# A sixth of a conditioning product moved from the first stage to the routing stage, in plain f32, and a first norm scaled in four chunks

## What is computed

```python
mod = jax.nn.silu(c) @ w_ada + b_ada            # c: 9 vectors of 2048; w_ada: 2048 x 12288
sh1, sc1, gt1, sh2, sc2, gt2 = split(mod, 6)
h  = rms_norm(x, g_pre_mix) * (1 + sc1) + sh1   # the first norm
z  = h @ w_in                                   # then gated linear attention, a conv branch, and a merge: mix
x  = x + gt1 * rms_norm(mix, g_post_mix)
h2 = rms_norm(x, g_pre_ffn) * (1 + sc2) + sh2
f  = peer(h2, ...)                              # product keys: top 16 of 128 twice, top 16 of their sums, experts
x  = x + gt2 * rms_norm(f, g_post_ffn)
```

## Time and profile before

| what | value |
|---|---|
| median of 3 runs | 5565.51 us (5557.96, 5565.51, 5580.36) |
| profiled execution, span from first to last instruction | 5572.9 us |
| profiled execution's own time | not listed apart; of the three runs only 5580.36 us is as long as that span, 7.5 us above it |
| PE, DVE, ACT, POOL busy | 90%, 61%, 31%, 25% of the span |
| bytes moved by DMA | 1334.66 MB, 239 GB/s on average |
| first stage | 0 to about 342 us |
| routing stage | about 2970 to 3209 us |

### The profile page before, as it was taken

The page is one execution under the profiler, slowest core; times in us unless marked ns, Lnnn a source line. Parts: engine busy times, 40 slices in busy tenths (PEclk is TensorE's granted clock), DMA queues, the critical chain, the costliest instruction groups (busy, mean ns, idle before and its releaser), DMA issues. The chain is left out here.

```text
span 5572.9 us, 61778 instructions
## 1 busy us (share of the span) xinstructions
PE 5025.0 (90%) x23369; PEld 4105.5 (74%) x23369; DVE 3416.3 (61%) x4470; ACT 1727.9 (31%) x2279; POOL 1402.2 (25%) x1059
## 2 busy tenths in 40 slices
PE   8989999999998888989793589999999999978885
PEld 3347888888886545868683589999999889866774
DVE  7842211115675243222558968888888778878898
ACT  6843112122223111122424623333333233323332
POOL 0500000000100131000004723333434333444453
PEclk9989999999999899989897899999999999999998
DMA  9842322233333355432511699999999999999998
GB/s 362 321 155 89 104 96 99 88 104 101 114 101 119 133 205 192 154 109 90 168 38 35 147 350 382 394 376 379 374 373 380 370 377 372 388 381 406 407 400 347
DMA packets 460055, 1334.66 MB, mean 239 GB/s; under 512 B 135868, under 2 KB 193084, under 8 KB 377198
## 3 DMA queue, kind: packets, MB, share of 16 engines
q1 hardware_dynamic: 336180, 667.06, 33.9%
q0 software_dynamic: 96576, 623.69, 28.5%
q10 hardware_dynamic: 27072, 40.91, 2.1%
HBM read 1206.06 MB, written 126.56 MB: 239 GB/s over the span
## 5 line engine op out<-in xcount | busy, mean ns | idle before, releaser
L229 PE MATMUL ps<-w_hi,act_hi 128*128 128x512 f32 x3040 | 1202.0, 395 | 36.6 <-DVE w_lo L224 16.3
L230 PE MATMUL ps<-w_lo,act_hi 128*128 128x512 f32 x3040 | 1191.9, 392 | 0.0
L231 PE MATMUL ps<-w_hi,act_lo 128*128 128x512 f32 x3040 | 1191.7, 392 | 0.0
L224 DVE TENSOR_TENSOR w_lo<-w_stage,w_hi 128x2048 fp32r<-128x2048 f32 x152 | 348.2, 2291 | 1134.6 <-ACT w_hi L220 1133.8
L2436 ACT ACTIVATE x_hi<-x_stage 128x1024 fp32r<-128x1024 f32 x512 | 543.4, 1061 | 1504.8 <-DMA x_stage<-u_turned 707.5
L2526 DVE TENSOR_TENSOR x_lo<-x_stage,x_hi 128x1024 fp32r<-128x1024 f32 x512 | 626.2, 1223 | 368.7 <-ACT x_hi L2436 368.1
L2363 POOL DMA_INDIRECT u_ring<-u_exp,idx_all x256 | 597.1, 2332 | 844.4 <-DVE u_ring L2544 801.5
L2390 PE MATMUL ps<-act_hi,x_hi 128*128 128x384 f32 x2048 | 697.3, 340 | 60.2 <-DVE x_lo L2526 57.4
L2390 PE MATMUL ps<-x_hi,cx_hi 128*128 128x512 f32 x1536 | 611.8, 398 | 99.7 <-DVE cx_lo L2537 82.8
L229 PEld LDWEIGHTS ps<-w_hi,act_hi 128*128 128x128 f32 x3040 | 576.2, 190 | 162.0 <-issue 32.1
L2391 PE MATMUL ps<-act_lo,x_hi 128*128 128x384 f32 x2048 | 694.4, 339 | 0.0
(11 more groups left out here) (315 smaller groups left out, 5637.3 us busy)
## 6 DMA issues: line engine op xcount, KB each, us to landing
x_stage<-u_turned SPq DMA_DIRECT2D x256, 512.0 KB, 8.6
x_stage<-v_exp SPq DMA_DIRECT2D x256, 512.0 KB, 9.3
w_stage<-w_ada SPq DMA_DIRECT2D x96, 1024.0 KB, 6.1
w_stage<-w_in SPq DMA_DIRECT2D x96, 1024.0 KB, 5.2
d_w<-w_buf SPq DMA_DIRECT2D x6, 4096.0 KB, 20.7
gwr<-d_w SPq DMA_DIRECT2D x128, 192.0 KB, 10.6
d_gw<-gob ACTq DMA_DIRECT2D x128, 192.0 KB, 6.9
gwr<-d_gw SPq DMA_DIRECT2D x128, 192.0 KB, 10.3
```

Of the source, the lines that this page charges most:

```text
L224: dve.tensor_tensor(w_lo[:, q % 2], w_in_st[:, q], w_hi[:, q % 2].bitcast(F32), ALU.subtract).then_inc(w_split, 1)
L229: pe.matmul(out, lhs[0], rhs[0], start=first, stop=False)
L230: pe.matmul(out, lhs[0], rhs[1], start=False, stop=False)
L231: return pe.matmul(out, lhs[1], rhs[0], start=False, stop=last)
```

## The change

The first stage makes 20 chunks, not 24, in the order first shift, first scale, second shift, second scale, first gate (`PARTS`, `place`). The first norm's scaling is packed into chunks 14 to 17, four blocks in each. SCALE2 moves to chunk 16. The conditioning vectors, after silu, are stored to DRAM (`d_c`).

The routing stage makes the last sixth: four chunks of 512 columns, each in eight halves of a quarter (`HALVES` = 32; a half is 256 rows x 512 columns, 512 KB). PE multiplies the weights as they come, in plain f32, with no split by ACT or DVE: two matmuls a half, and one with a single row for the bias after each eighth half. There are two buffers, and the load of half n waits until half n - 2 was multiplied; the first load of a new chunk waits for the whole chunk before it. 24 halves stand on PE ahead of everything else of the stage, the other 8 one behind each of the first eight groups of tile 0. When all 32 are used, the gain's rows are loaded; DVE multiplies them with the sums in PSUM after its last tile, and SP writes the result to `d_post`.

```diff
-    NA = 6 * D // NCOL
+    NA = 5 * D // NCOL
+    PARTS = (0, 1, 3, 4, 2)
...
-        SCALE0, TURN0, MT, AFF0, POST1, SCALE2 = 7, 8, 10, 14, 12, 20
+        SCALE0, TURN0, MT, AFF0, SCALE2 = 7, 8, 10, 14, 16
...
-            return range(2 * (c - AFF0), 2 * (c - AFF0) + 2) if AFF0 <= c < AFF0 + KD // 2 else ()
+            return range(4 * (c - AFF0), 4 * (c - AFF0) + 4) if AFF0 <= c < AFF0 + KD // 4 else ()
+        def place(c):
+            return PARTS[c // 4] * 4 + c % 4
...
-            pool.dma_start(mod[:], a["b_ada"].broadcast_to([NSEQ, 6 * D])).then_inc(s_b, 16)
+            pool.dma_start(mod[:], a["b_ada"][:, 0:5 * D].broadcast_to([NSEQ, 5 * D])).then_inc(s_b, 16)
...
+            pool.wait_ge(s_csplit, 1)
+            pool.dma_start(d_c, c_in[:]).then_inc(s_modout, 16)
...
-            pool.dma_start(d_mod, mod[:]).then_inc(s_modout, 16)
+            pool.dma_start(d_mod[:, 0:5 * D], mod[:]).then_inc(s_modout, 16)
...
-                if not ks or j % 2 == 0:
+                if not ks:
                     return
-                k = ks[j // 2 % 2]
+                k = ks[j % QPC]
...
-                if ks and n % (2 * QPC) in (3, 6):
-                    k = ks[n % (2 * QPC) // 6]
+                at = n % (2 * QPC)
+                if ks and at in (2, 3, 5, 6):
+                    k = ks[(2, 3, 5, 6).index(at)]
...
+        G2 = 4
+        HALVES = 2 * QPC * G2
+        EARLY = 24
...
         @block.sync
         def _(sp):
+            sp.dma_start(c_all[:], d_c).then_inc(g2_c, 16)
+            for n in range(HALVES):
+                i, h = divmod(n, 2 * QPC)
+                if h == 0:
+                    if i > 0:
+                        sp.wait_ge(g2_sum, i)
+                    at = 5 * D + i * NCOL
+                    sp.dma_start(b_row[:], a["b_ada"][:, at:at + NCOL]).then_inc(g2_b, 16)
+                if n >= 2:
+                    sp.wait_ge(g2_used, n - 1)
+                src = a["w_ada"][(5 * D // NCOL + i) * QPC + h // 2]
+                sp.dma_start(wst[:, n % 2], src[:, h % 2 * (QK // 2):(h % 2 + 1) * (QK // 2), :]).then_inc(g2_in[n % 2], 16)
+            sp.wait_ge(g2_used, HALVES)
+            sp.dma_start(g_rows, a["g_post_ffn"].broadcast_to([NSEQ, D])).then_inc(g2_g, 16)
...
+            sp.wait_ge(g2_done, G2)
+            sp.dma_start(d_post, g_rows).then_inc(g2_out, 16)
...
+            sp.wait_ge(g2_out, 16)
...
+            def gate_half(n):
+                i, h = divmod(n, 2 * QPC)
+                if n == 0:
+                    pe.wait_ge(g2_c, 16)
+                pe.wait_ge(g2_in[n % 2], 16 * (n // 2 + 1))
+                for kk in range(QK // 2):
+                    k = h * (QK // 2) + kk
+                    mm = pe.matmul(ps[0:NSEQ + 1, i], c_all[:, k], wst[:, n % 2, kk], start=k == 0, stop=False)
+                mm.then_inc(g2_used, 1)
+                if h == 2 * QPC - 1:
+                    pe.wait_ge(g2_b, 16 * (i + 1))
+                    pe.wait_ge(g2_ones, 1)
+                    pe.matmul(ps[0:NSEQ + 1, i], ones[:], b_row[:],
+                              start=False, stop=True).then_inc(g2_sum, 1)
+            for n in range(EARLY):
+                gate_half(n)
             for t in range(ND):
                 turn_ids(t)
                 for q in range(NQ):
                     spread(t, q)
+                    if EARLY + t * NQ + q < HALVES:
+                        gate_half(EARLY + t * NQ + q)
...
+            dve.wait_ge(g2_sum, G2)
+            dve.wait_ge(g2_g, 16)
+            for i in range(G2):
+                g = g_rows[:, i * NCOL:(i + 1) * NCOL]
+                dve.tensor_tensor(g, ps[0:NSEQ, i], g, ALU.mult).then_inc(g2_done, 1)
```

More of the change, by code:

```diff
@@ L169, in _build @@
     d_post = d_mod[:, 5 * D:6 * D]
+    d_c = dram("d_c", (P, KD, NSEQ + 1))
     kc_at = -(-nc.sbuf_base // 32) * 32
@@ L266, in _build @@
     with stage() as (st, block):
-        c_in = sb(st, "c_in", [P, KD, NSEQ])
-        c_sig = sb(st, "c_sig", [P, KD, NSEQ])
+        c_in = sb(st, "c_in", [P, KD, NSEQ + 1])
+        c_sig = sb(st, "c_sig", [P, KD, NSEQ + 1])
         c_hi = sb(st, "c_hi", [P, KD, NSEQ + 1], F32R)
         c_lo = sb(st, "c_lo", [P, KD, NSEQ + 1], F32R)
-        mod = sb(st, "mod", [NSEQ, 6 * D])
+        mod = sb(st, "mod", [NSEQ, 5 * D])
         g9 = sb(st, "n1_g9", [NSEQ, D])
@@ L300, in _ @@
                 for q in range(QPC):
-                    load_quarter(sp, c, q, a["w_ada"][c * QPC + q])
+                    load_quarter(sp, c, q, a["w_ada"][place(c) * QPC + q])
             for q in range(QPC):
@@ L322, in _ @@
                 pool.tensor_tensor(rows_k, rows_k, by_stream[0], ALU.add).then_inc(h_sample, 1)
-            for n, name in ((1, "g_pre_ffn"), (2, "g_post_ffn")):
-                pool.wait_ge(gain_done, n + 1)
-                pool.dma_start(g9[:], a[name].broadcast_to([NSEQ, D])).then_inc(s_g9, 16)
+            pool.wait_ge(gain_done, 2)
+            pool.dma_start(g9[:], a["g_post_mix"].broadcast_to([NSEQ, D])).then_inc(s_g9, 16)
             pool.wait_ge(m2_taken, 1)
             pool.dma_start(d_mod2t, mod_t[:].rearrange("p m k s -> p (m k s)")).then_inc(s_modout, 16)
-            pool.wait_ge(gain_done, 4)
-            pool.dma_start(d_mod, mod[:]).then_inc(s_modout, 16)
-            pool.wait_ge(s_modout, 32)
+            pool.wait_ge(gain_done, 3)
+            pool.dma_start(d_mod[:, 0:5 * D], mod[:]).then_inc(s_modout, 16)
+            pool.wait_ge(s_modout, 48)
         @block.scalar
@@ L425, in extras @@
                                     ).then_inc(mt_taken, 1)
-                if c == POST1 or c == NA - 1:
-                    n, at = (1, 2 * D) if c == POST1 else (3, 5 * D)
-                    dve.wait_ge(s_g9, 16 * (n + 1))
+                if c == NA - 1:
+                    dve.wait_ge(s_g9, 48)
                     dve.wait_ge(mod_read, c + 1)
-                    dve.tensor_tensor(mod[:, at:at + D], mod[:, at:at + D], g9[:], ALU.mult).then_inc(gain_done, 1)
+                    dve.tensor_tensor(mod[:, 2 * D:3 * D], mod[:, 2 * D:3 * D], g9[:], ALU.mult).then_inc(gain_done, 1)
                 if c == SCALE2:
-                    dve.wait_ge(s_g9, 48)
+                    dve.wait_ge(s_g9, 32)
                     dve.wait_ge(mod_read, c + 1)
@@ L511, in _ @@
                 if c == SCALE2 + 1:
-                    pe.wait_ge(gain_done, 3)
+                    pe.wait_ge(gain_done, 2)
                     pe.wait_ge(m2_clear, 1)
@@ L1948, in _build, with route @@
     lk = link(None, "dve")
-    route(nc, a, stage, sem, sb, kc, ps, (idx_all, wt_all, top_all, topi_all), area, d_w, lk)
+    route(nc, a, stage, sem, sb, kc, ps, (idx_all, wt_all, top_all, topi_all), area, d_w, lk, d_c, d_post)
     experts(nc, a, stage, sem, sb, ps, (idx_all, wt_all), act_hi, act_lo, area, d_post, d_w, d_gw, d_f3, d_x2, d_h2)
-def route(nc, a, stage, sem, sb, kc, ps, route_sb, area, d_w, lk):
+def route(nc, a, stage, sem, sb, kc, ps, route_sb, area, d_w, lk, d_c, d_post):
     idx_all, wt_all, top_all, topi_all = route_sb
@@ L1992, in route @@
         w_buf = sb(st, "w_buf", [P, 2, NKEY, P // 2])
+        c_all = sb(st, "g2_c", [P, KD, NSEQ + 1])
+        wst = sb(st, "g2_w", [P, 2, QK // 2, NCOL])
+        b_row = sb(st, "g2_b", [1, NCOL])
+        ones = sb(st, "g2_ones", [1, NSEQ + 1])
+        g_rows = wst[0:NSEQ].rearrange("p a k n -> p (a k n)")
+        G2 = 4
+        HALVES = 2 * QPC * G2
+        EARLY = 24
+        g2_ones = sem("g2_onesdone")
+        g2_c, g2_b, g2_in = sem("g2_cin"), sem("g2_bin"), [sem(f"g2_in{n}") for n in range(2)]
+        g2_used, g2_sum, g2_g, g2_done, g2_out = (sem("g2_" + n) for n in ("used", "sum", "gin", "done", "out"))
+        assert nc.sbuf_base <= 229344 - 4 * (2 * TT - 3) * NH * TOPK
         s_ex, s_exd, gate, route_done = sem("r_ex"), sem("r_exd"), sem("r_gate"), sem("r_done")
@@ L2031, in _ @@
                                  w_buf[:, h]).then_inc(w_out[h], 16)
+            sp.wait_ge(g2_done, G2)
+            sp.dma_start(d_post, g_rows).then_inc(g2_out, 16)
             for h in range(2):
                 sp.wait_ge(w_out[h], 16 * ND)
+            sp.wait_ge(g2_out, 16)
         @block.gpsimd
         def _(pool):
+            pool.memset(ones[:], 1.0).then_inc(g2_ones, 1)
             for t in range(ND):
@@ L2648, in layout @@
         "x": np.concatenate([f["x_prompt"].reshape(NP_TOK, D), f["x_sample"].reshape(NTOK - NP_TOK, D)], 0),
-        "cT": np.ascontiguousarray(c.T.reshape(KD, P, NSEQ).transpose(1, 0, 2)),
+        "cT": np.pad(c.T.reshape(KD, P, NSEQ).transpose(1, 0, 2), ((0, 0), (0, 0), (0, 1))),
         "w_ada": f["w_ada"][0].reshape(QPC, QK, P, 6 * D // NCOL, NCOL).transpose(3, 0, 2, 1, 4).reshape(-1, P, QK, NCOL),
```

11 lines of the change are left out of this document (4 added, 7 removed).

## The result

The changed kernel takes 5590.73 us (median of 5, 5582.69 to 5594.99); the kernel before, run beside it, 5566.07 (5557.96 to 5580.36). The ratio is 1.0035, 95% interval [1.0019, 1.0052]: slower by 19 us with an interval of 11 to 29 (the two medians differ by 24.7), about the half per cent that the prediction calls no change, and inside its range of 5548 to 5609. The profiled execution took 5583.85 us with a span of 5582.3, so 1.5 us lie around a span. (The table of the kernel before put 7.5 there by taking one of the three runs for the profiled one; it cancels in a difference.)

What follows compares the result with a forecast made beforehand. No single engine bounds the first stage (PE, DVE and ACT sums meet near 11.1 us a chunk); DVE bounds routing. -40 + 45 + 2 + 4.6 = +11.6 us, carried to a median of 5577 us, range 5548 to 5609.

Steps and rivals of the forecast that it cites:

- First stage, -40: First stage: four chunks fewer, norm packed in four, smaller bias load and last write; 40 us less, bounds -32 to -60.
- the 14 us that the prediction wanted to see in each: First stage, profile sign: ACT without idle time in chunks 14 to 17, each 14 us or more.
- The bias: First stage's start: the bias DVE waits for is 360 KB, not 432; 1.5 us less.
- rival 3: First stage gives back 55 to 60 us and PE is only 25 late: -28 or below, 5537 us; chance 0.07.
- PE late by 45: Routing stage: 24 halves through two buffers, 5.17 us per two, bring PE to tile 0 45 us late.
- the 3.2 of the estimate beside it: Routing stage: the skill's DMA formula estimates 3.2 us for a half's load, making PE 43 us late.
- All of the lateness is kept: Routing stage: DVE is the bound, so all of PE's 45 us of lateness lengthens the stage.
- Rival 4: Routing stage: the stall is absorbed; DVE's idle time in tiles 1 to 3 allows at most 9 of 45 us.
- Eight halves between groups, +2 (0 to 8): Routing stage, tile 0: a half behind each of eight groups costs PE time, partly hidden by DVE's lead; 2 us more.
- The end, +4.6: Routing stage's end: DVE's four gate operations, 2.5 us, then SP's 72 KB write; 4.6 us more.
- Rival 1: Routing stage: halves come slower, by loads of 5 us or more or half clock; 5597 or 5609 us; chance 0.24.
- Rival 2: Routing stage: loads overlap so PE never waits and is 25 us late; net -8, 5557 us; chance 0.16.

Runs made afterwards that it cites:

- e4_deep24: The changed kernel with its 24 halves ahead of tile 0 in eight buffers, not two, and the first three bias rows loaded at once: 5556.64 us, ratio 0.9973.
- g4_final16: The changed kernel with 16 halves ahead in eight buffers, 16 between, writes on ACT's queue, two bias buffers, gate multiplied before tile 3: 5543.02 us, ratio 0.9943.
- g1_act_writes: `f5_early8` with the six writes of `d_w` issued by ACT in place of SP: 5553.31 us, ratio 0.9965 to the kernel before.
- f5_early8: The changed kernel with 8 halves ahead of tile 0, 24 between groups, SP's loads and `d_w` writes merged in group order: 5577.92 us, ratio 1.0018.

## Why the prediction came out as it did

Its mechanism held, and the net was +20.3 in the two stages where it had +11.6. That the miss is only 9 us is in part luck: the first stage gave 5 us more than forecast and the routing stage took 14 more, and the two errors have opposite signs. Step by step:

- **First stage, -40: measured -45.1**, outside the prediction's own -34 to -44. The size of one term was off. ACT's chunk was summed from durations; the pitch between starts is 0.1 us less for each of 16 operations. The four packed chunks took 57.4 us, for 56.6 with 5.5 more for the scale and POOL. So the 14 us that the prediction wanted to see in each is met on the average and by luck: two are 12.6 and 12.7, and the two longer ones have what the sum left out or took too small (DVE slowed beside POOL; the scale and the wait for POOL in one chunk). The six are 80.6 for the predicted 85.8. The bias gave 1.3 of 1.5. The prediction's rival 3 rested on this doubt, but the whole of it was worth 5 us, not 15 to 20. (Its -28 is the sum for 60 us given back; 55 make -23.)
- **PE late by 45: measured 60.** This is the term that was mis-sized most; it is why the stage grew by 65.4 and not by 52. A half took 2.93 us in the steady part (2933.71 to 2948.38, five halves), not 2.59: loads landed after 3.9 us and not the 3.4 that was the least among the loads into `x_stage` (the 3.2 of the estimate beside it was further off), the matmuls are 1.81, and the two with the hand-overs are 5.87 for two halves. 24 halves: +8. The rest is at the chunks' ends and at the slow start. From PE's first half to its transposes (2926.09, 2955.36, 2984.40, 3009.20) the three chunks took 29.3, 29.0 and 24.8 us, where the prediction's terms give 23.4, 23.4 and 21.6: 14.7 of the 15 us. With eight buffers (`e4_deep24`) the transposes come 51.4 us after the stage's start (2971.51 - 2920.11), in place of 87.9.
- **All of the lateness is kept**: right. DVE is idle for 59.79 us in one piece, and the stage is longer by that and the end. Rival 4 had nothing: behind that wait the stage is 5.8 us longer than before, the end's 5.3 among them.
- **Eight halves between groups, +2 (0 to 8)**: 1.3 in tile 0, and 0.5 over the stage. That it was so cheap hid a limit: a tile has 16 groups, and DVE is busy with it for some 58 us (62.1 less its wait of 3.78). PE's tile is 16 x 3.35 = 53.6 before, 57.2 with eight halves, and 60.8 with sixteen, to which come two bias rows (1.9), a first group and half at the clock's lower level (2.2) and the two waits for loads (2.2): 67.2 in `g4_final16` (2962.12 to 3029.31). Somewhere between eight and sixteen halves PE comes to set the tile's pace. In `g1_act_writes`, also with sixteen in tile 0, the wait of 7.29 us for a load comes on top.
- **The end, +4.6**: 5.3.
- **Rival 1** has the amount nearly right (it decides for slower from a lateness of 61 on, and 60 came), but neither of its reasons is what happened. Loads were 3.9, not 5, and the clock in the three windows was 0.83, 0.89 and 0.94. The Trainium skill, "TensorE: Matmul & The Clock Gate", HAM oscillation, has a kernel throttled again by its waits for DMAs, which are some 3 to 5 us each. That is not this case, and the prediction should not have counted it for the rival: here waits of about 1 us in each half, and two of 2.13 and 2.46, did not do that, the records behind them being 1.89 for four. Some matmuls ran at the lower level at the stage's start (5.49 for eight records) and behind the two waits at a chunk's start (4.14 and 4.15; 6.21 and 5.30 for eight), which agrees with the page.
- **Rival 2**, PE sets the pace, is false for two buffers and true for eight, by `e4_deep24`: DVE's wait is 23 us there, for the rival's 25.

The runs of fewer halves ahead refuted my own next theory, that the cost is only what stands ahead of tile 0: moving the halves behind it met SP's queue first, and PE's pace and the loads beside a write second. How much of the 16.44 us is the queue and how much the engines being full (0.96 busy at 231 GB/s from 2999 to 3018 us) is told by `g1_act_writes` only in part: the same write is then in flight, the issue is not held, and the largest landing is 8.9 us. Why the issue is held no run shows.

## What to carry to other kernels

Work that is put ahead of the first tile of a pipeline is paid in full, however small its share of the engine, if the engine that sets the pace needs that tile at once: count when the first hand-over comes, not the busy share. With a stream that is multiplied as it lands, two buffers give a pace of half of landing plus work (here 3.9 and 1.8 us, and a pace of 2.93); ask for enough buffers that the work alone is left, and let no load wait for a chunk's end. Loads that are spread through a stage want a queue of their own beside bulk writes, and the filler of an idle engine is free only up to the slack of one tile. When a wait is read as a cost, take off what the same wait was before.

## What the runs showed of the hardware that was not expected

- A load issued on SP's queue behind a write of 4 MB in pieces of 256 bytes was held at its issue for 16.44 us, and one of 72 KB for 18.50 (`f5_early8`); with the write on ACT's queue the longest issue was 1.16, and the loads landed in 4.0 in the median and 8.9 at most. The Trainium skill, "DMA: Bandwidth & Descriptors", Queues, rings and completion order, says that SP and ACT have rings of their own and that a DMA engine takes turns between them packet by packet; the landings in `g1_act_writes` agree. The hold at the issue itself is this trace's.
- Plain f32 with ten columns stationary and 512 moving costs 0.90 us a matmul (1.81 for a half), four times a rounded one's 0.23, and the fewer stationary columns made it no cheaper than the 0.885 with 128.
- In the first stage PE's clock also fell for a few matmuls after a wait of 2.07 us (0.90 in the chunk of 242 to 259 us), while in the routing stage waits of 1 us in every half, and two of 2.13 and 2.46, left it at the upper level.
- DVE and POOL slow each other both ways. Beside a DVE without gaps a POOL operation lasted 12.3 us and more, and beside a POOL that made its operations one after another DVE's subtractions took 1.42 and 1.02 us for 1.21 and 0.80.
